# FFN: block products that add up in two PSUM bank chains, down tiles between the products, three bank pairs

## The reference

```python
def conv_ffn(h, w_up, conv_w, conv_b, w_down):        # h: 1024 x 1024, d_ff = 2816
    u = h @ w_up                                       # gate and value, 2 x 2816 columns
    u = causal_depthwise_conv(u, conv_w, width=3) + conv_b
    gate, val = jnp.split(u, 2, axis=-1)
    return (jax.nn.silu(gate) * val) @ w_down
```

## Time and profile before

| | us |
|---|---|
| median of 3 runs | 2634.8 (2634.44 to 2636.25) |
| span of the profiled execution | 2631.1 |
| from the span to the median | 3.7 |
| first product of unit 3 to first product of unit 21, layer 0 and layer 1 | 565.75, 565.76 |
| from there to the end of the layer's sums of squares | 60.96, 57.13 |

### The profile page before, as it was taken

How to read it: one execution, slowest core, us unless ns; L and a number is a source line. 1 busy time by engine, 2 the same in 40 slices (tenths; PEclk the granted TensorE clock), 3 DMA queues, 4 the chain that set the end, 5 groups by cost and what they waited for, 6 DMA issues and landing times.

```text
span 2631.1 us, 31515 instructions
## 1 busy us (share of the span) xinstructions
PE 2439.2 (93%) x11916; PEld 1957.4 (74%) x11916; DVE 1926.0 (73%) x2195; ACT 846.4 (32%) x1439; POOL 1462.1 (56%) x1123
## 2 busy tenths in 40 slices
PE   7899999989999999996899999978989999999993
PEld 5688887777777777773677787757777777777772
DVE  3676673796888888789666777662796788888878
ACT  3344451451111111114346465652441111111112
POOL 2222114547888888884441323114546888888883
PEclk9999999999999999998999999978999999999997
DMA  4122134401111111122121212043311111111112
GB/s 153 56 65 73 60 134 152 147 30 57 49 49 48 57 49 61 52 88 102 53 65 39 87 52 80 18 160 120 128 57 51 54 49 48 49 57 48 57 63 104
DMA packets 51236, 191.97 MB, mean 73 GB/s; under 512 B 5904, under 2 KB 6416, under 8 KB 47376
## 3 DMA queue, kind: packets, MB, share of 16 engines
q1 hardware_dynamic: 39184, 148.92, 17.1%
q10 hardware_dynamic: 11904, 41.05, 4.1%
HBM read 146.43 MB, written 29.36 MB: 67 GB/s over the span
## 4 chain that ended last, share of the span: by engine, by line
PE 73%; DVE 16%; ACT 4%; issue 3%; DMA 2%; SPq 1%; ACTq 0%; POOL 0%; POOLq 0%; DVEq 0%
PE ps L1208 9%; PE ps L1209 9%; PE ps L1210 9%; PE ps L1230 6%; PE ps L1231 6%; PE ps L1232 6%; PE ps L1039 3%; PE ps L1011 2%; PE ps L1013 2%; PE ps L1012 2%; PE ps L1076 2%; PE ps L1056 2%; PE ps L1131 1%; PE ps L996 1%; PE ps L1133 1%
## 5 line engine op out<-in xcount | busy, mean ns | idle before, releaser
L2079 DVE TENSOR_TENSOR a<-a,ps 128x1024 f32<-128x1024 f32 x336 | 409.4, 1220 | 196.7 <-PE ps L1232 188.5
L748 POOL CAST w_hi<-w_raw 128x1024 fp32r<-128x1024 f32 x78 | 84.9, 1088 | 801.8 <-PE ps L1013 274.8
L1230 PE MATMUL ps<-hid,ring 128*128 128x512 f32 x704 | 294.7, 419 | 30.0 <-DVE a L2079 16.7
L1575 ACT ACTIVATE cy<-cx,cv 128x1024 f32<-128x1024 f32 x76 | 94.8, 1247 | 675.4 <-DVE cx L2050 675.4
L830 POOL TENSOR_TENSOR ring<-w_raw,ring 128x512 fp32r<-128x512 f32 x206 | 298.6, 1449 | 16.5
L1231 PE MATMUL ps<-hid,ring 128*128 128x512 f32 x704 | 278.1, 395 | 0.0
L1232 PE MATMUL ps<-hid,ring 128*128 128x512 f32 x704 | 277.0, 393 | 0.0
L828 POOL CAST ring<-w_raw 128x512 fp32r<-128x512 f32 x206 | 167.9, 815 | 184.2 <-PE ps L1232 92.8
L1209 PE MATMUL ps<-h,ring 128*128 128x512 f32 x608 | 237.2, 390 | 0.0
L1208 PE MATMUL ps<-h,ring 128*128 128x512 f32 x608 | 237.1, 390 | 0.0
L1210 PE MATMUL ps<-h,ring 128*128 128x512 f32 x608 | 236.8, 389 | 0.0
(11 more groups left out here) (274 smaller groups left out, 6504.1 us busy)
## 6 DMA issues: line engine op xcount, KB each, us to landing
w_raw<-in_W SPq DMA_DIRECT2D x166, 512.0 KB, 3.2
raw_d<-in_W SPq DMA_DIRECT2D x44, 512.0 KB, 3.2
h<-o_dram ACTq DMA_DIRECT2D x2, 6144.0 KB, 21.2
x_dram<-x ACTq DMA_DIRECT2D x6, 2048.0 KB, 7.3
x<-x_dram SPq DMA_DIRECT2D x2, 4096.0 KB, 13.3
dsw<-draw SPq DMA_DIRECT2D x64, 128.0 KB, 2.3
o_dram<-most SPq DMA_DIRECT2D x6, 1024.0 KB, 4.9
o_dram<-dost SPq DMA_DIRECT2D x6, 1024.0 KB, 4.5
```

Source lines behind the costliest of these rows:

```text
L1230: pe.matmul(out, wh, xh, start=True, stop=False)
L2079: dve.tensor_tensor(a[:, f, :], a[:, f, :], src, ALU.add).then_inc(acc_done, 1)
```

## The change

- PE's order of the products becomes P1, P2, P6, P5, P7, P3, P4. They no longer have a bank each. P1, P6, P7 and P4 add up in one bank without a new start flag, P5 and P3 in another, in which P2 stood before. So the bank holds P1, then U2 = P1 + P6, then U2 + P7, then C21; the other P2, then P5, then P5 + P3. The two banks change places from unit to unit.
- Four reads of the banks are ScalarE copies to `cx` (behind P1, P6, P5, P4), three are VectorE adds (P2, P7, P3). Each product waits for the read of what its bank held.
- `cx` and, from unit 1 on, `hid` exist once. `hid_top` of unit n waits for the last tile of unit n-1.
- The down tiles use three bank pairs (2 to 7) and stand between the products: P1, tile 6 of unit n-2, P2, tile 7 of unit n-2, P6, P5, tiles 0 and 1 of unit n-1, P7, tiles 2 and 3, P3, tile 4, P4, tile 5. In unit 3 all 8 tiles of unit 1 stand around P2; in unit 21 tiles 4 to 7 of unit 20 stand behind P4.
- Items, loads and the orders of VectorE and ScalarE follow. Value tile and gate tile of the convolution change places.

```diff
-PRODUCTS = ["P1", "P6", "P2", "P5", "P7", "P4", "P3"]
+PRODUCTS = ["P1", "P2", "P6", "P5", "P7", "P3", "P4"]
...
+CHAIN = {"P1": 0, "P6": 0, "P7": 0, "P4": 0, "P2": 1, "P5": 1, "P3": 1}
+OPENS = ["P1", "P2", "P5"]
+COPIED = ["P1", "P6", "P5", "P4"]
+ADDED = ["P2", "P7", "P3"]
...
+        old = [("dn", n - 2, f) for f in (range(KT) if n == PLAIN else range(6, KT))]
+        new = [("dn", n - 1, f) for f in range(KT)]
+        p1, p2, p6, p5, p7, p3, p4 = [("up", n, c) for c in PRODUCTS]
+        half = len(old) // 2
+        out += [p1] + old[:half] + [p2] + old[half:] + [p6, p5]
+        if n < HT - 1:
+            out += new[0:2] + [p7] + new[2:4] + [p3] + new[4:5] + [p4] + new[5:6]
         else:
-            out += ups[:-1] + tiles[:1] + ups[-1:] + tiles[1:]
+            out += new[0:2] + [p7] + new[2:3] + [p3] + new[3:4] + [p4] + new[4:]
...
+        out += [(n, "S2"), (n, "S1"), (n - 1, "d1"), (n, "S3"), (n, "S4"), (n - 1, "d2"), (n, "V2")]
...
-        cx = at("cx", 42, 4)
+        cx = at("cx", 42, 2)
...
         def up_bank(n, name):
-            return bank((len(PRODUCTS) * (n - PLAIN) + PRODUCTS.index(name)) % 4)
+            return bank((n - PLAIN + CHAIN[name]) % 2)
+        def down_bank(n, f):
+            return 4 + 2 * (f % 2) if n == 0 else 2 + 2 * ((KT * (n - 1) + f) % 3)
+        def hid_part(n, low):
+            return hid[:, (2 if n else 0) + low, :]
...
                     elif n < HT:
-                        sp.wait_ge(item_ready, item_count(layer, n - 1, "V2"))
-                        load_ffn(layer, n, "V")
                         sp.wait_ge(item_ready, item_count(layer, n - 1, "S4"))
                         load_ffn(layer, n, "G")
...
+                    if PLAIN < n < HT:
+                        sp.wait_ge(item_ready, item_count(layer, n - 1, "V2"))
+                        load_ffn(layer, n, "V")
...
+                    before = {"P1": "P3", "P2": "P4", "P6": "P1", "P5": "P2", "P7": "P6", "P3": "P5", "P4": "P7"}[name]
+                    wait_read(pe, layer, n - 1 if name in ("P1", "P2") else n, before)
...
-                        pe.matmul(out, wh, xh, start=k == 0, stop=False)
+                        pe.matmul(out, wh, xh, start=k == 0 and name in OPENS, stop=False, skip_group_check=True)
...
-                        pe.wait_ge(acc_done, acc_count(layer, n, f) - 2)
+                        pe.wait_ge(acc_done, acc_count(layer, n, f) - 3)
...
+            def bank_copy(layer, n, name):
+                v, half = {"P1": (0, 0), "P6": (0, 1), "P5": (1, 1), "P4": (1, 0)}[name]
+                act.wait_ge(up_done, up_count(layer, n, name))
+                if n == PLAIN:
+                    act.wait_ge(dn_done, down_count(layer, 0, KT - 1))
+                else:
+                    act.wait_ge(conv_done, conv_count(layer, n - 1, v))
+                act.activation(half_of(cx, v, half), up_bank(n, name), ACT.Copy).then_inc(bank_copied, 1)
...
+                    if n >= 2:
+                        act.wait_ge(dn_done, down_count(layer, n - 1, KT - 1))
+                    act.activation(hid_part(n, 0), cy[:, 0, :], ACT.Copy).then_inc(hid_hi, 1)
...
                 for n in range(PLAIN, HT):
                     if n > PLAIN:
+                        gate(n - 1)
+                    bank_copy(layer, n, "P1")
+                    hid_top(n - 1)
+                    bank_copy(layer, n, "P6")
+                    bank_copy(layer, n, "P5")
+                    act.wait_ge(bank_added, added_count(layer, n, "P3"))
                     act.wait_ge(hid_lo, u0 + n)
                     tap(n, 0)
+                    bank_copy(layer, n, "P4")
+                    act.wait_ge(bank_copied, copied_count(layer, n, "P4"))
+                    tap(n, 1)
...
+                def bank_add(n, name):
+                    v, half, copied = {"P2": (0, 0, "P1"), "P7": (1, 1, "P5"), "P3": (0, 1, "P6")}[name]
+                    dst = half_of(cx, v, half)
+                    dve.wait_ge(up_done, up_count(layer, n, name))
+                    dve.wait_ge(bank_copied, copied_count(layer, n, copied))
+                    dve.tensor_tensor(dst, dst, up_bank(n, name), ALU.add).then_inc(bank_added, 1)
...
                 for n in range(PLAIN, HT):
+                    if n == PLAIN:
+                        for f in range(4):
+                            add(1, f)
+                    else:
                         conv_tile(n - 1, 1)
+                        product(n - 1)
+                        add(n - 2, 6)
+                    bank_add(n, "P2")
+                    for f in range(4 if n == PLAIN else 7, KT):
+                        add(n - 2, f)
                     hid_tail(n - 1)
+                    add(n - 1, 0)
+                    add(n - 1, 1)
+                    bank_add(n, "P7")
+                    add(n - 1, 2)
                     if n < HT - 1:
+                        add(n - 1, 3)
+                    bank_add(n, "P3")
+                    if n < HT - 1:
+                        add(n - 1, 4)
+                        conv_tile(n, 0)
+                        add(n - 1, 5)
+                    else:
+                        add(n - 1, 3)
+                        conv_tile(n, 0)
                 conv_tile(HT - 1, 1)
                 product(HT - 1)
                 add(HT - 2, 4)
                 hid_tail(HT - 1)
-                for f in range(6, KT):
+                for f in range(5, KT):
                     add(HT - 2, f)
```

More of the change, by code:

```diff
@@ L94, in weight_items @@
         if n == PLAIN:
-            out += [(n, c) for c in ("G1", "S2", "G2", "S1")] + [(1, "d1"), (1, "d2"), (n, "S3")]
+            out += [(n, "G1"), (1, "d1"), (n, "G2"), (1, "d2")]
         else:
[L97 to L101, removed]
+            out += [(n, "G1"), (n, "G2")]
+        out += [(n, "S2"), (n, "S1"), (n - 1, "d1"), (n, "S3"), (n, "S4"), (n - 1, "d2"), (n, "V2")]
     return out + [(HT - 1, "d1"), (HT - 1, "d2")]
@@ L581, in conv_count @@
         def conv_count(layer, n, v):
-            return 2 * (HT * layer + n) + 1 + (v if n < PLAIN else 1 - v)
+            return 2 * (HT * layer + n) + 1 + v
         def down_count(layer, n, f):
@@ L1182, in plain_units, with bank_free @@
                             plain_part(1, part, k)
-                def bank_free(n, place):
-                    if n == PLAIN and place < 4:
-                        pe.wait_ge(conv_done, conv_count(layer, PLAIN - 1, place // 2))
+                def bank_free(n, name):
+                    if n == PLAIN and name in ("P1", "P2"):
+                        pe.wait_ge(conv_done, conv_count(layer, PLAIN - 1, 0))
                         return
[L1189 to L1195, removed]
+                    before = {"P1": "P3", "P2": "P4", "P6": "P1", "P5": "P2", "P7": "P6", "P3": "P5", "P4": "P7"}[name]
+                    wait_read(pe, layer, n - 1 if name in ("P1", "P2") else n, before)
                 def product(n, name):
@@ L1201, in product @@
                     pe.wait_ge(item_ready, item_count(layer, n, WEIGHT_OF[name]))
[L1202 removed]
+                    bank_free(n, name)
                     for k in range(KH):
@@ L1207, in product @@
                         _, xh, xl = combination(c, k)
-                        pe.matmul(out, wh, xh, start=k == 0, stop=False)
-                        pe.matmul(out, wh, xl, start=False, stop=False)
-                        last = pe.matmul(out, wl, xh, start=False, stop=k == KH - 1)
+                        pe.matmul(out, wh, xh, start=k == 0 and name in OPENS, stop=False, skip_group_check=True)
+                        pe.matmul(out, wh, xl, start=False, stop=False, skip_group_check=True)
+                        last = pe.matmul(out, wl, xh, start=False, stop=k == KH - 1, skip_group_check=True)
                     last.then_inc(up_done, 1)
@@ L1227, in down @@
                     for half in range(2):
-                        out = bank(4 + 2 * (f % 2) + half)
-                        xh, xl = half_of(hid, 2 * (n % 2), half), half_of(hid, 2 * (n % 2) + 1, half)
+                        out = bank(down_bank(n, f) + half)
+                        tok = slice(half * HB, (half + 1) * HB)
+                        xh, xl = hid_part(n, 0)[:, tok], hid_part(n, 1)[:, tok]
                         pe.matmul(out, wh, xh, start=True, stop=False)
@@ L1602, in ffn @@
                 tap(0, 1)
-                gate_and_split(0)
+                gate(0)
+                hid_top(0)
                 act.wait_ge(up_done, up_count(layer, 1, "g1"))
```

96 lines of the change are left out of this document (25 added, 71 removed).

## The result

The median of the changed kernel is 2595.28 us (2589.48 to 2595.64, 4 runs) beside 2635.53 (2634.44 to 2640.72, 4 runs) of the kernel before: ratio 0.9842, 95% interval 0.9828 to 0.9856. The profiled execution has a span of 2593.2 us, 37.9 less than before.

The account below looks back on a forecast made before the run. PE was taken to bound the kernel, busy 93%, losing 16.2 us a layer to waits for VectorE's adds. -18.95 x 2 + 3.3 + 4.1 = -30.5 us from 2634.8 gave 2604.3 (predicted 2604.5), range 2599 to 2616.

Parts of the forecast that it names:

- Unit 3: ... I find no wait: Start of unit 3: items and sums run before P1, needed banks are freed before 588, so no wait.
- 590.65: Time in us at which P1 of unit 3 starts, d2(1) and the sums having run before it.
- Bounds: Range check: slowest VectorE steps beside GpSimd give 2633 us, fastest gain nothing more; a fallen tail clock gives 2606 to 2608.
- The stretch: P1(3) to P1(21), each layer: units of 29.92 us without stalls, 565.75 falling to 546.8, 18.95 us less.
- the steady unit's 0.81 us: Loss in each 30.73 us unit before the change, where down tiles in a row wait for VectorE's adds into `a`.
- The narrow places: Steady unit: `hid_tail` ends 1.6 us before t0 wants it; P2's add has 1.9 us of slack before P5.
- Rival C: Single `hid` buffer: d7, `hid_top`, `hid_tail`, t0 have 5.4 us cover; 2 us late gives 2676 us; chance 0.05.
- the 0.85 us of the prediction: Delay of t0 per unit beyond which the single `hid` buffer makes the kernel slower than before.
- B: VectorE holds P2's add and `hid_tail`; stalls of 0.2 to 0.6 us a unit, 2611 to 2626 us; chance 0.12.
- The tail: P1(21) to last sum of squares: 64.3 and 61.2 us against 60.96 and 57.13, costing 3.3 and 4.1.
- so I take none: Tail, PE's rests before t7 and dn(21, 0): no clock loss counted, at most some 2 us a layer.
- from the span to the median: Median of runs 2634.8 lies 3.7 us above the profiled span 2631.1, taken as unchanged.

Follow-up runs that it names:

- experiment 1: Changed kernel with unit 3's three GpSimd sums back ahead of the split of G1: 2609.27 us, 0.9903 of the kernel before.
- experiment 2: Kernel before with only the changed kernel's unit 3 start order of items and sums: 2626.72 us, 0.9966 of the kernel before.
- experiment 3: Changed kernel with two bank pairs for the down tiles in place of three, unit 21's tile 5 add ahead of `hid_tail`: 2605.25 us, 0.9886.
- experiment 7: Changed kernel with the four bank copies made by VectorE in place of ScalarE: 2602.47 us, 0.9879 of the kernel before.
- Experiment 4: Changed kernel with bank chains and three bank pairs, but down tiles in a row as in the kernel before: 2600.56 us, 0.9872.
- experiment 6: Changed kernel with `hid_tail` writing the low part twice more in units 3 to 20: 2662.15 us, 1.0102 of the kernel before.
- experiment 5: Changed kernel with `hid_tail` writing the low part once more in units 3 to 20: 2608.55 us, 0.9905 of the kernel before.
- experiment 8: Changed kernel with unit 21's tile 4 add before conv_tile(21, 1) and tile 5's before `hid_tail`: 2586.50 us, 0.9807 of the kernel before.

## Why the prediction was wrong, point by point

**The failed step** is "Unit 3: ... I find no wait", and with it the place of P1(3), "590.65", taken over from before. The diff moves unit 3's sums behind (1, "d1"), (1, "d2"). I asked only whether the moved items would be ready for their products, not what GpSimd ran beside in the old order. The sums, and the splits that they pushed back, ran beside VectorE's token differences and `hid_tail`, for which PE's third down tile waits by way of ScalarE. It was worth 6.91 + 6.40 us, shown by experiments 1 and 2 from both sides. The rows for it were at hand: the window 572.90 to 579.60 in the earlier trace rows shows VectorE busy for 6.70 of 6.70 us and GpSimd for 3.40, with PE at 0.36, and the next window has the clock at 0.53. I used it for the clock alone.

The exclusion of GpSimd and VectorE that "Bounds" weighs (the Trainium skill, SBUF — State Buffer, "SBUF: two separate sides") fits what acts here: where both inputs of VectorE lie in SBUF, 5.52 us for four differences beside GpSimd and 2.48 without. The trace agrees; the prediction applied it to the steady units, where it cost PE nothing, and not to the start. One reading in "Bounds" was loose: the step of 1.36 that it took for one without a split (912.67) still overlaps one of GpSimd's (911.65 to 912.94), and steps beside no GpSimd work take 1.27 to 1.28. That changes no sum.

**The stretch** (18.95 forecast, 19.03 and 19.04 measured) was right: 29.92 a unit, the clock at 1.00 throughout, no down tile waiting in units 4 to 20. What it was due to is narrower than I thought: by experiment 3 the third bank pair has no part in the steady unit's 0.81 us, and experiment 7 shows that neither has the work taken off VectorE. What is left is the places of the tiles, with VectorE's order that goes with them. No run puts tiles between products that keep a bank each, so whether the bank chains are needed for 29.92 stays open. Experiment 4 gives the third pair with the chains 0.34 of 0.81 us a unit, when the tiles stay in a row.

**The narrow places** were named rightly: `hid_top` and `hid_tail` before t0, with 2.07 us (1.6 forecast). I had taken 3.3 us a convolution; the one shown took 2.8 (1.27 and 1.51), the other of the unit 3.3; product and `hid_tail` did meet a split (2.12, 2.01). Rival C's mechanism is real: with 1.91 us of delay a unit experiment 6 is 28 us slower than the kernel before. Its point of crossing is not the 0.85 us of the prediction but 40/36 = 1.1, since the start gave 13 us more. It was not reached, nor was B.

**The tail** was priced at +3.3 and +4.1 and measured at +4.67 and +4.45. The changed kernel's rows, layer 0 and (from 2534) layer 1:

```profile
1167.02 1.21 DVE L2096 TENSOR_TENSOR a<-a,ps 128x1024 f32<-128x1024 f32 x1
1168.28 0.80 PE L1249 MATMUL ps<-hid,ring 128*128 128x512 f32 x1 [2.99 <-DVE a L2096]
1168.88 0.63 PE L1250 MATMUL ps<-hid,ring 128*128 128x512 f32 x1
1171.31 1.06 ACT L1609 ACTIVATE hid<-cy 128x1024 fp32r<-128x1024 f32 x1 [7.23 <-PE ps L1251]
1172.40 1.23 DVE L2086 TENSOR_TENSOR hid<-cy,hid 128x1024 fp32r<-128x1024 f32 x1 [4.17 <-ACT hid L1609]
1177.18 0.91 DVE L2150 MEMSET ss<- 128x1024 f32 x1 [0.16 <-issue]
...
2534.91 0.50 PE L1249 MATMUL ps<-hid,ring 128*128 128x512 f32 x1 [2.99 <-DVE a L2096]
2535.24 0.40 PE L1250 MATMUL ps<-hid,ring 128*128 128x512 f32 x1
2536.66 1.06 ACT L1609 ACTIVATE hid<-cy 128x1024 fp32r<-128x1024 f32 x1 [5.95 <-PE ps L1251]
2542.53 0.91 DVE L2150 MEMSET ss<- 128x1024 f32 x1 [0.17 <-issue]
```

t7 starts 34.43 us behind P1(21) in both layers (34.3 forecast), the memset stands at +43.33 and +42.05 (41.9 forecast), and from it to the end it takes 22.30 and 19.53 (22.4 and 19.3). The step that was mis-sized is the clock, "so I take none": in layer 0 it fell in the rest before t7, its six matmuls stand 0.43 apart (the first 0.59) instead of 0.23 (0.34), and from the start of t7 to `hid_top` it takes 3.03 us in layer 0 and 1.75 in layer 1: 1.28 of the 1.4 missing. In layer 1 the same rest left the clock up. There the forecast is right to 0.35. Behind the other rest, before dn(21, 0), the clock fell in both layers, which cost next to nothing: VectorE is the path there, and from the memset on the times are the forecast's to 0.3.

**The sum, put right:** 2604.3 - 13.3 (the stage ahead of unit 3) - 0.2 (stretches) + 1.7 (tails) + 4.35 (all else) - 1.6 (from the span to the median it is 2.1 us, not 3.7) = 2595.3. The 4.35 us of all else are drift, not forecast, and they hid part of the miss: without them the time would lie near 2591. The range was too narrow since it held only the costs that I had named.

## What to carry to other kernels

When a diff moves an item in one engine's list, ask at both places what it runs beside and which items it pushes back, here GpSimd's beside VectorE's, not only whether it is ready in time; a stage that the change "does not touch" deserves a window of its own, above all where PE rests and another engine is busy throughout. In this kernel a tile of work that frees its banks slowly was better set between long products (29.92 a unit with two pairs) than given more banks (30.4 with three). And an add whose data is ready belongs ahead of any chain that PE waits for: moving two adds of the tail took 7.6 us off the two tails.

## What was not expected of the hardware

- The clock after a rest of PE is not settled by the rest's length alone. The same wait of 2.99 us before t7 (3.4 between the starts of two matmuls) stands in eight layers of four runs: the change and experiments 1, 5 and 6. In six of them the matmuls behind it stood 0.43 us apart (the 1.2 GHz level); in layer 1 of the change and layer 0 of experiment 6 they stood 0.23 apart (2.4 GHz). In experiment 7 (waits of 4.01) the clock stayed up for the first matmuls behind the rest and then fell. In experiment 8, behind waits of 3.48 and 3.47 before unit 21's first tile, it stayed up over the next twelve matmuls in layer 0 and fell after about six in layer 1. Behind a wait of only 1.83 in unit 3 of experiment 2 it fell after about six matmuls in layer 0, and behind 1.84 it stayed up in layer 1. What decides it stays open.
- The adds that read PSUM did not slow down beside GpSimd: 1.21 to 1.22 us in all 311 cases of the changed kernel, where a product with both inputs in SBUF took 1.23 without GpSimd and 1.77 to 2.31 beside it.
- A stall cost PE more than its length: in experiment 5 t0 was 0.24 us late and the unit 0.36 longer, in every unit from 4 to 20.
